# Keys and values from their own input buffers, a third slot of split weights, and compressed scores beside the heads' scores

## The reference, cut to what matters

```python
s = rmsnorm(stream, kv_norm_g)                       # stream: 256 x 1024, after the first layer
kv = s @ kv_w                                        # six parts of 2 groups x 64: two to compress, k and v selected, k and v of the window
blk = tok[:, :, idx] + pos                           # 15 windows of 32 tokens, stride 16
k_cmp = silu(blk.reshape(..., 2048) @ w1) @ w2       # the same for v_cmp
h = rmsnorm(x, norm_g) * (1 + scale) + shift
proj = h @ in_w                                      # q (1024), z (3072), gates (48)
s_c = q @ k_cmp + bias;  p_c = masked_softmax(s_c);  o_c = p_c @ v_cmp      # 16 heads, 15 compressed keys
s_s, s_w = q @ k_sel + bias, q @ k_win + bias        # 16 heads, causal over 256 tokens; softmax and @ v each
y = sum over the three branches of gates * o * silu(z);  x = x + gate * (y @ out_w)
```

## Time and profile before

| What | Value |
|---|---|
| Time, median of 3 runs | 1169.79 us (1168.8 to 1179.2) |
| Time of the profiled execution | 1172.15 us |
| Its span, first to last instruction | 1170.3 us |
| PE busy | 1077.6 us |
| DVE busy | 709.5 us |
| ACT busy | 582.7 us |
| POOL busy | 102.2 us |
| Mean granted TensorE clock | 0.976 |

### The profile page before, as it was taken

How to read it: one execution, slowest core, us unless ns; L and a number is a source line. 1 busy time by engine, 2 the same in 40 slices (tenths; PEclk the granted TensorE clock), 3 DMA queues, 4 the chain that set the end, 5 groups by cost and what they waited for, 6 DMA issues and landing times. The chain is left out here.

```text
span 1170.3 us, 17304 instructions
## 1 busy us (share of the span) xinstructions
PE 1077.6 (92%) x7252; PEld 965.3 (82%) x7252; DVE 709.5 (61%) x1029; ACT 582.7 (50%) x875; POOL 102.2 (9%) x94
## 2 busy tenths in 40 slices
PE   2699998899978999999899989999998969999997
PEld 2599887798967878887888879998887958998996
DVE  5779774776454665466546656545546785555554
ACT  3354545724555454444456655344445775444344
POOL 1100018270000001112000000000000200000000
PEclk9999999999989999889899999999999989999999
DMA  9766335542326862202443335555554434555551
GB/s 321 226 186 177 127 109 155 169 141 81 112 77 213 267 238 73 73 1 73 144 144 108 109 122 188 194 180 181 182 188 135 144 107 150 196 185 190 181 180 72
DMA packets 118349, 178.43 MB, mean 152 GB/s; under 512 B 5156, under 2 KB 78018, under 8 KB 118272
## 3 DMA queue, kind: packets, MB, share of 16 engines
q1 hardware_dynamic: 116736, 172.40, 45.6%
q0 software_dynamic: 1120, 2.97, 0.8%
q10 hardware_dynamic: 416, 1.97, 0.4%
HBM read 176.27 MB, written 1.05 MB: 152 GB/s over the span
## 5 line engine op out<-in xcount | busy, mean ns | idle before, releaser
L1250 DVE TENSOR_TENSOR sb_w_lo<-sb_raw,sb_w_hi 128x2048 fp32r<-128x2048 f32 (+2 forms) x141 | 320.3, 2271 | 249.7 <-ACT sb_w_hi L629 249.6
L629 ACT ACTIVATE sb_w_hi<-sb_raw 128x2048 fp32r<-128x2048 f32 (+2 forms) x141 | 266.1, 1888 | 171.1 <-PE G L2032 131.3
L2030 PE MATMUL X<-sb_hT_hi,sb_w_hi 128*128 128x256 f32 x992 | 285.0, 287 | 13.7 <-DVE sb_hT_lo L1574 9.1
L2032 PE MATMUL X<-sb_hT_hi,sb_w_lo 128*128 128x256 f32 x992 | 282.2, 284 | 0.0
L2031 PE MATMUL X<-sb_hT_lo,sb_w_hi 128*128 128x256 f32 x992 | 282.0, 284 | 0.0
L2030 PEld LDWEIGHTS X<-sb_hT_hi,sb_w_hi 128*128 128x128 f32 x992 | 191.6, 193 | 17.2 <-DVE sb_hT_lo L1574 9.5
L2031 PEld LDWEIGHTS X<-sb_hT_lo,sb_w_hi 128*128 128x128 f32 x992 | 191.6, 193 | 0.7
L2032 PEld LDWEIGHTS X<-sb_hT_hi,sb_w_lo 128*128 128x128 f32 x992 | 191.5, 193 | 0.0
L2030 PE MATMUL G<-sb_w_hi,sb_uT_hi 128*128 128x512 f32 x272 | 108.3, 398 | 0.8 <-DVE sb_w_lo L1250 0.8
L2031 PE MATMUL G<-sb_w_lo,sb_uT_hi 128*128 128x512 f32 x272 | 107.6, 396 | 0.0
L2032 PE MATMUL G<-sb_w_hi,sb_uT_lo 128*128 128x512 f32 x272 | 107.6, 396 | 0.0
(11 more groups left out here) (420 smaller groups left out, 1755.6 us busy)
## 6 DMA issues: line engine op xcount, KB each, us to landing
sb_raw<-in_mlp_w SPq DMA_DIRECT2D x64, 1024.0 KB, 5.4
sb_raw<-in_ada_w SPq DMA_DIRECT2D x24, 1024.0 KB, 5.3
sb_raw<-in_a_in_w SPq DMA_DIRECT2D x16, 1024.0 KB, 5.9
sb_raw<-in_b_in_w SPq DMA_DIRECT2D x16, 1024.0 KB, 5.8
sb_raw<-in_sb_w_qkv SPq DMA_DIRECT2D x12, 1024.0 KB, 5.2
sb_raw<-in_rg_w_in SPq DMA_DIRECT2D x8, 1024.0 KB, 5.7
sb_raw<-in_a_out_w SPq DMA_DIRECT2D x4, 1024.0 KB, 5.0
sb_raw<-in_b_out_w SPq DMA_DIRECT2D x4, 1024.0 KB, 5.1
```

The lines of the kernel that those rows point to most:

```text
L629: nc.scalar.activation(w_hi[s][:, 0:nk * w], raw[b % RAW_SLOTS][:, 0:nk * w], ACT.Copy).then_inc(S["w_hi"], 1)
L1250: nc.vector.tensor_tensor(w_lo[s][:, 0:nk * w], raw[b % RAW_SLOTS][:, 0:nk * w], w_hi[s][:, 0:nk * w].bitcast(F32), ALU.subtract).then_inc ...
L2030: dt32(out, lh, rh, start=first, stop=False, skip_group_check=shared)
L2032: return dt32(out, ll, rh, start=False, stop=last, skip_group_check=shared)
```

## The change

Nothing of the mathematics is changed. The parts:

- **Own input buffers.** `kvT_hi` and `kvT_lo` hold the input of the key and value products. The transposes of `h1` and their split no longer wait for these products and come right after block 0; they use the four G banks. DVE's intermediate goes to `xn` in place of `tpair`.
- **Key and value blocks.** Block 1 now has the keys of both branches (48 matmuls of 256 columns), block 2 the values of both (48 of 256). Each of these two blocks is loaded by two transfers of 128 columns, whose rows in memory are 512 bytes in place of 1024.
- **Copies to POOL.** The 8 copies into `tok2` and the 8 into `kdup` go from ACT to POOL, each 64 partitions x 256. DVE's windows wait for `tok2`; the first scores wait for `kdup`.
- **A third slot.** `w_hi2` and `w_lo2` lie in the memory of `kvT`, from the first query block's successor to the last block ahead of z. In this stretch block m waits for PE to have used block m - 3.
- **Another order.** Query and compression blocks alternate, by `B_ORDER`: q0 q1 k0 q2 k1 q3 v0 v1.
- **Compressed scores.** For heads 0 to 7 `scores(h)` also computes the compressed scores of heads 2h and 2h + 1, in columns 384 to 443 of bank G0: two matmuls of 30 columns, against `kc_T`, which now has both halves of the partitions with zeros between (POOL clears it). DVE adds the bias right behind `nmx` (8 instructions of 60 columns in place of 4 of 120). The next scores on PE wait for that too. `c_shift`, `c_scale`, `c_weights_T` and `c_out` come one head earlier each.

```diff
-        TR_BANK = TB + G[2:4]
+        TR_BANK = {"h0": TB + G[2:4], "h1": G}
+        slot, last_in = {}, {}
+        three = range(first_mm["b_q"], first_mm["b_z"])
+            elif m in three:
+                slot[m] = ((three[0] % 2), 2, 1 - three[0] % 2)[(m - three[0]) % 3]
@@ weight transfers, SP
+                if loads(b) == 2:
+                    for half in range(2):
+                        cs = slice(half * P, (half + 1) * P)
+                        sp.dma_start(dst[:, :, cs], src[half]).then_inc(S[f"raw_in{s}"], 16)
@@ POOL
+            pool.wait_ge(S["kv_raw"], 1)
+            for i in range(2):
+                for g in range(BG):
+                    src = tpair[0][g * HD:(g + 1) * HD, i, :]
+                    ch.mark(nc.gpsimd.tensor_copy(tok2[i][0:HD, g, :], src))
+                    ins = nc.gpsimd.tensor_copy(tok2[i][HD:P, g, 0:T - 1], src[:, 1:T])
+                ins.then_inc(S["tok2"], 1)
+            pool.wait_ge(S["kv_raw"], 2)
+            for br in range(2):
+                for g in range(BG):
+                    for half in range(2):
+                        ins = nc.gpsimd.tensor_copy(kdup[br][half * HD:(half + 1) * HD, g, :],
+                                                    tpair[1][g * HD:(g + 1) * HD, br, :])
@@ split_hi, ACT
-                if m >= SPLIT_SLOTS:
-                    act.wait_ge(S["w_used"], m - SPLIT_SLOTS + 1)
+                if before[m] >= 0:
+                    act.wait_ge(S["w_used"], before[m] + 1)
+                if m == three[1]:
+                    act.wait_ge(S["w_used"], last_mm["kv"] + 1)
@@ DVE, beside the heads
+            def c_scores(pair):
+
+                heads = slice(2 * pair, 2 * pair + 2)
+                nc.vector.tensor_tensor(pc[:, :, heads, :].rearrange("p q h n -> p q (h n)"),
+                                        G[0][:, 3 * P:3 * P + 4 * NCMP].rearrange("p (q n) -> p q n", q=MT),
+                                        bias_cmp[:, :, heads, :].rearrange("p q h n -> p q (h n)"), ALU.add).then_inc(S["c_bias"], 1)
@@ PE
-            for br in range(2):
-                bank = X[(1 + br) % 2]
-                    passes(bank[:, 0:T], (hi[:, k, 0:P], lo[:, k, 0:P]), hT(k), k == 0, k == KC - 1)
-                        ins = passes(bank[:, T + m * P:T + (m + 1) * P], hT(k, m), (hi[:, k, P:T], lo[:, k, P:T]),
+            transposes("h1")
+            _, hi, lo = take()
+                    ins = passes(X[1][:, c * T:(c + 1) * T], (hi[:, k, cs], lo[:, k, cs]), hT(k, call="kv"), k == 0, k == KC - 1)
+            _, hi, lo = take()
+                    ins = passes(X[0][:, m * T:(m + 1) * T], hT(k, m, "kv"), (hi[:, k, :], lo[:, k, :]), k == 0, k == KC - 1)
+            for name in B_ORDER:
+                if name[0] == "q":
+                    query_block(int(name[1]))
+                else:
+                    compression("kv".index(name[0]), int(name[1]))
@@ PE, scores(h)
                 if h >= 1:
                     pe.wait_ge(S["nmx"], h)
+                    pe.wait_ge(S["c_bias"], min(h, 8))
+                if h < 8:
+                    ins = c_scores(h)
```

More of the change, by code:

```diff
@@ L156, in weight_blocks @@
             out_half("a_out", I["a_out_w"][0], n // 2)
-    for n in range(3):
-        feature_major("kv", I["kv_w"], n * 256)
+    feature_major("kv", I["kv_w"], 0)
+    kv_w = I["kv_w"].rearrange("(c p) n -> p c n", p=P)
+    for first in (256, 384):
+        out.append(("mm", "kv", (kv_w[:, :, first:first + P], kv_w[:, :, first + 256:first + 256 + P]), KC, 256))
     b_in = I["b_in_w"][0]
     feature_major("b_gate", b_in, 4 * D, 3 * BH)
[L161 to L165, removed]
+    for name in B_ORDER:
+        if name[0] == "q":
+            feature_major("b_q", b_in, int(name[1]) * 256)
+        else:
+            w = "cmp_k_w1" if name[0] == "k" else "cmp_v_w1"
+            rows(w, I[w], slice(0, CMP_HID), 8 * int(name[1]), 8)
     for j, n in enumerate(Z_ORDER):
@@ L474, in gain, with loads, loaded, parts @@
             return param(gain_cols[call])[:, k:k + 1]
+        slot, last_in = {}, {}
+        three = range(first_mm["b_q"], first_mm["b_z"])
+        for m in range(len(mm_raw)):
+            if m < three[0]:
+                slot[m] = m % SPLIT_SLOTS
+            elif m in three:
+                slot[m] = ((three[0] % 2), 2, 1 - three[0] % 2)[(m - three[0]) % 3]
+            else:
+                slot[m] = (1 - slot[three[-2]], slot[three[-2]])[(m - three[-1] - 1) % 2]
+        before = {}
+        for m, s_ in slot.items():
+            before[m] = last_in.get(s_, -1)
+            last_in[s_] = m
+        def loads(b):
+            return 2 if isinstance(blocks[b][2], tuple) else 1
+        def loaded(b):
+            return 16 * sum(loads(i) for i in range(b % RAW_SLOTS, b + 1, RAW_SLOTS))
+        def parts(call):
+            return (kvT_hi, kvT_lo) if call == "kv" else (hT_hi, hT_lo)
         def slot_view(t, b):
@@ L915, in _ @@
-            ins.then_inc(S["fm_out"], 1)
-            for br in range(2):
[L917 to L930, removed]
@@ L1318, in shifted_lo @@
                     ch.settle()
-                    nc.vector.tensor_tensor(hT_lo[:, 2 * g:2 * g + 2, :], tpair[g % 2][:, :, :],
+                    nc.vector.tensor_tensor(hT_lo[:, 2 * g:2 * g + 2, :], whole,
                                             hT_hi[:, 2 * g:2 * g + 2, :].bitcast(F32), ALU.subtract)\
@@ L2500, in scores, with c_scores @@
                     ins = dt32(bank[:, P:3 * P], qB[r, h // 2, P:T], kdup[br][r, g, :], start=True, stop=True)
+                if h < 8:
+                    ins = c_scores(h)
                 ins.then_inc(S["s_head"], 1)
+            def c_scores(pair):
+                for q in range(MT):
+                    o = 3 * P + q * 2 * NCMP
+                    ins = dt32(G[0][:, o:o + 2 * NCMP], qB[:, pair, q * P:(q + 1) * P], kc_T[:, pair // 4, :], start=True, stop=True)
+                return ins
             def first_scores():
                 pe.wait_ge(S["fm_out"], 19)
+                pe.wait_ge(S["kdup"], 1)
                 pe.wait_ge(S["tm_out"], 2 + 3)
+                pe.wait_ge(S["cmp_k"], 2)
                 scores(0)
```

239 lines of the change are left out of this document (123 added, 116 removed).

## The result

The changed kernel takes 1154.49 us (median of 4 runs, 1152.97 to 1156.19), the kernel before 1169.3; the ratio is 0.986 (0.983 to 0.989). The forecast was 1148.0 with a range of 1139 to 1159. The time lies in the range; the gain is 15 us in place of 22, and the parts of the sum were wrong in both directions, as the traces show.

A forecast was written before the change was run, and what follows sets the result against it. PE, busy 1077.6 of 1170.3 us, bounds the kernel. 14.8 us less from key and value products to z and 6.9 in the heads make 21.7: 1172.15 becomes 1150.4, the median 2.4 lower, 1148; range 1139 to 1159.

The forecast's parts named there:

- Key and value blocks: Both blocks, 16.91 us before, become 96 matmuls of 256 columns, 11.6 us: 4.9 us less.
- The wait for `h1` and the slow gates: Ahead of and in the gates' 24 matmuls: the 7.4 us wait and 2.8 us of slow clock go, 10.2 us less.
- Waits and half clock of the compression blocks: Compression among the queries: two waits (3.9 us) and a block at half clock go, 5.4 us less.
- I count half a copy for each of the first six ... 2.5 us there: 4.0 us: POOL's copies hold up DVE: 1.5 us over six instructions, 2.5 us at the windows, 4.0 us in all.
- All are split ahead of need: Query and compression blocks with three slots and the new order: every block split in time, the nearest being z0 (0.7 us).
- DVE's chain is exactly as long as PE's: At q0, DVE's split and PE both at 323.9 us, so whatever lengthens DVE's chain is paid by PE.
- 5.7 less, if the small matmuls are the reason: Heads 9 and 10, behind the compressed scores: 14.64 us at low clock become 8.94 at full clock.
- the stop of 1.3 us ahead of head 9's output products: PE waits 1.3 us in head 9, as DVE copies head 9's weights behind a split, gated heads and factors.
- at q0 it had allowed 1.5 us: One block at half clock behind PE's 3.5 us wait at q0, 1.5 us added.
- heads 9 and 10 slow down anyway: Rival, chance 0.13: clock falls because the dense z pieces end with head 7; 5.7 us stay, 1154.
- a low clock after head 8: Sign of being wrong; the forecast expected clock 1.00 through heads 8 to 10, each below 6 us.
- POOL copies over 0.7 us: Sign of being wrong; the forecast took 0.5 us for each copy on POOL.

The follow-up runs named there:

- late_h1: late_split with the transposes of `h1` behind the two key and value blocks, as before the change; 1155.62 us.
- late_two: late_split with two slots of split weights in place of three; 1152.4 us.
- act_copies: The changed kernel with the 16 copies back on ACT in place of POOL; 1153.12 us.
- filled_stop: The changed kernel with six matmuls of 512 columns, result unread, put ahead of head 9's output products, where PE stopped; 1147.13 us.
- late_split: The changed kernel with the split of a block of output weights (ACT and DVE) moved from after head 8 to after head 11; 1147.38 us.
- late_order: late_split with three slots but the blocks in the order of before (q0 to q3, then k0, k1, v0, v1); 1146.09 us.
- two_slots: The changed kernel with two slots of split weights all along, in the new order of blocks; 1155.0 us.

## Why the prediction was right and wrong

**Right in size.** Key and value blocks: 11.48 us in place of 16.91, 5.4 less with the row of norms that moved out of it; forecast 4.9. This is read from the windows; no run takes this part back. The wait for `h1` and the slow gates: 9.6 us by late_h1; forecast 10.2. Waits and half clock of the compression blocks: 34.14 us for what took 23.13 + 16.89, 5.9 less, and 5.8 by late_two; forecast 5.4. But the forecast put it down to slots and order together, and it is the slots alone.

**Wrong: the copies on POOL.** The step "I count half a copy for each of the first six ... 2.5 us there: 4.0 us" failed. POOL's timeline of the changed kernel, with DVE's split of 128x2048 running from 311.04 to 313.51:

```profile
310.97 0.40 POOL L629 COPY sb_tok<-sb_tpair 64x256 f32<-64x256 f32 x1
311.43 2.35 POOL L630 COPY sb_tok<-sb_tpair 64x255 f32<-64x255 f32 x1
313.83 0.39 POOL L629 COPY sb_tok<-sb_tpair 64x256 f32<-64x256 f32 x1
```

A copy takes 0.39 us, and 2.35 beside the split. Of the eight copies of the keys the median took 0.57 us and the longest, beside q0's split, 2.34. The engines do shut each other out, but here it is POOL that pays: DVE's split took 2.47 us in place of 2.29, its windows 2.64 in place of 2.26. The earlier trace rows had said so: the split beside the add of 3.26 us took its usual 2.28. I read from them that there is contention and not who bears it.

POOL doesn't always pay. In the long instructions of these rows it is the one that starts second that waits for the end of the first. The copy of 311.43 started 0.4 us behind the split and ended 0.3 us behind it; the add of 3.26 us started 0.16 us behind its split. In the kernel before, near 919 us, it is the other way round:

```profile
918.97 1.29 POOL L613 TENSOR_TENSOR sb_ii<-sb_ii,sb_xc 128x512 f32<-128x512 f32 x1 [3.59 <-ACT sb_ii L1174]
919.11 3.30 DVE L1250 TENSOR_TENSOR sb_w_lo<-sb_raw,sb_w_hi 128x2048 fp32r<-128x2048 f32 x1
```

The add, 0.14 us ahead, took its usual time, and the split 1.0 us more than its 2.28. What DVE can lose to one copy is the rest of it, below 0.4 us, where POOL can lose a whole split; the forecast charged half a copy of 0.5 us to each of six instructions, though the eight copies for the windows were done at 315.9, ahead of four of the six, and 2.5 us to the windows. DVE's whole loss was 0.6 us: from the start of block 2's split to the end of the windows it took 12.7 us, and 12.1 in act_copies. So 0.9 us of wait came in place of 4.2 (by the forecast's own chains 4.0, since 323.9 + 4.0 is 3.3 us behind 323.9 + 0.7), and no half clock; and the 0.9 us are not the copies', as the next paragraph shows.

**Wrong: what is late at q0.** "All are split ahead of need" and "DVE's chain is exactly as long as PE's" missed the real bound. ACT's timeline of the changed kernel:

```profile
322.25 1.92 ACT L696 ACTIVATE sb_w_hi<-sb_raw 128x2048 fp32r<-128x2048 f32 x1 [5.23 <-PE X L2083]
325.01 0.38 ACT L792 ACTIVATE sb_r_row<-G 48x256 f32<-48x256 f32 x1 [0.84 <-PE G L2083]
```

and DVE's:

```profile
321.11 2.64 DVE L1692 TENSOR_TENSOR sb_win<-sb_tok,sb_params 128x120 f32<-128x120 f32 x8
324.21 2.35 DVE L1300 TENSOR_TENSOR sb_w_lo<-sb_raw,sb_w_hi 128x2048 fp32r<-128x2048 f32 x1 [0.46 <-ACT sb_w_hi L696]
```

q0's split goes into the slot of block 2, the last of the key and value blocks. ACT, idle for 5.2 us, may start it only when PE has used that block, at 322.2; 1.9 + 2.4 us later it is there, and the gates in between last only 3.4. DVE's windows end before that, and DVE itself waits 0.46 us for ACT. In act_copies this is 1.2 us, and PE waits as long as before.

**Wrong: the heads.** "5.7 less, if the small matmuls are the reason" named a true reason and not the only one. The forecast computed the stop of 1.3 us ahead of head 9's output products (1.32 measured) and charged 1.3 us for it. At the gates it had read from the earlier trace rows that a stop is followed by slow matmuls, and at q0 it had allowed 1.5 us for that; here it did not ask. Of the rivals the one at 1154, "heads 9 and 10 slow down anyway", was nearest in time, but its reason, the end of the dense z pieces, fell with filled_stop. Of the signs that the forecast gave for being wrong, two came: a low clock after head 8, and POOL copies over 0.7 us. What the compressed scores are worth from z on (143.7 us against 146.6 to 154.3 in the kernel before) is to be had with the split behind head 11.

**Not foreseen.** The rest of the program took 3.9 us more in the profiled execution, some 3 in the mean over all profiles.

Together: 5.2 us more than forecast in the first stretch, 6.9 less in the second, 3.9 less elsewhere: 21.7 + 5.2 - 6.9 - 3.9 = 16.1. The median came into the range partly because two errors of opposite sign met.

The best kernels here are late_split and late_order, 1147 and 1146 us, 7 to 8 below the changed kernel.

## What to carry to other kernels

Where an edit removes one cause of a low clock, look on the same engine, at the same place, for another: a stop that costs 1.3 us by itself cost 3.0 to 7.7 with what followed it. Move late-needed work off the engine that PE is about to wait for, or let PE do something in the gap. When two engines contend in a trace, read the start and the duration of both instructions, since the one that started first may pay nothing. And compare stretch by stretch: the time of two_slots hid a loss of 5 us behind a lucky clock elsewhere.

## What the runs showed of the hardware

Two triggers brought the lower clock in the heads: 64 instructions of 15 columns with PE busy throughout (in all five profiles that have them), and a stop of 1.32 us among products of 64 to 256 columns (in all four). A stop of 0.70 us among the same products, at 507.17 us of the changed kernel, did not, nor did one of nearly the same length (1.29 us), with eight transposes ahead of it, between two blocks of 512 columns; the window of the changed kernel that holds it:

```profile
512.24:530.98 18.74, 17.45 (x81) 14.37 (x81) 13.63 (x23) 8.15 (x11) 3.66 (x2) 1.00 0.18 57
```

Heads as light as head 9 run at 1.00 in the changed kernel once the clock is back, from 489.6 us in head 11 on. How long it stays low behind the same trigger differs from execution to execution: from z to the end of head 15 the kernel before took 146.6, 151.4 and 154.3 us. Where VectorE and GpSimd met in long instructions, the one that started second waited for the first to end: a GpSimd copy of 0.39 us took 2.35 behind a split, and a split of 2.28 us took 3.30 behind a GpSimd add.
